# A hybrid streaming layer on one core: DVE instead of POOL takes the remainders of fourteen weight blocks behind the attention slots

## The chip, the cores and the metric

The kernel runs on one core of one Trainium2 chip. The metric is the device time of one execution in microseconds (us); lower is better. The engines are named as in the profile: PE multiplies matrices, PEld is its weight load, DVE is the vector engine, ACT the scalar engine, POOL is GpSimd, SP issues the transfers.

## The reference

One layer of an encoder serves two groups with the same weights: 512 new tokens without a past, and 64 tokens with 256 cached ones, together T = 576 columns of width 1024. Cut to the part around the change:

```
mixed = concat(rms_norm(fox_o, g_fox_out), rms_norm(mla_o, g_mla_out))
x = x + mixed @ w_o
q = (rms_norm(x, g_mem) @ w_mq)          # 4 heads x 128
s = q . mem_k * MEM_SCALE                # 256 memory tokens
o = softmax(s) @ mem_v
x = x + o @ w_mo
hf = rms_norm(x, g_ffn)
x = x + (silu(hf @ w_gate) * (hf @ w_up)) @ w_down
```

where mem_k and mem_v of the prompt are rms_norm(mem, g_mem_src) @ w_mk and @ w_mv. Before this stand the two attentions (fox_o and mla_o). All is float32 in and out.

## The kernel before, in words

**High and low parts.** Every float32 product is made of three passes of PE at the rounded type fp32r: high by high, high by low, low by high (`product`, L460 to L462). So each operand x needs a rounded copy (ACT) and the remainder x minus its rounded copy (DVE or POOL).

**Weight blocks.** The front weights come as 49 blocks of up to 128 x 1024 columns. SP loads block b into `wraw[b % 2]` (`load`, L2295) as soon as the remainder of block b - 2 is made (`f_lo` at b - 1). ACT rounds it into `whi[b % 3]` (`split`, waits for the load and for PE to be done with block b - 3, counts `f_hi`). `rest(b)` on POOL (L2125) makes the remainder `wlo[b % 3]` and counts `f_lo`. PE waits for `f_lo` at b + 1 before it uses block b. Blocks are taken in order.

**The stage around the change.** The attentions run in 96 ticks (to about 315 us in the profile); their last blocks are 31 and 32. Behind them stand, in PE's order: `mixed(0..7)`, the second half of w_o, two m to a block (blocks 32, 34, 36, 38), `memory_keys(3)` (33), `memory_values(0..3)` (35, 37, 39, 41), the first two heads' queries (40, 42), and then 20 slots of the memory attention (5 row tiles x 4 heads) with the queries of heads 2 and 3 (43, 44) and parts of `memout` (45 and on) as filler. After the slots come memout's blocks to 48 and the feed-forward part.

**DVE's order there.** For each m of the loop over `mixed`: scale the product in PSUM by the row factors (L1835), add it to `xa` (L1837), which counts `r_x`; then `low2(m - 1)` (L1818, the low part of the normed input; for m of 1 to 4) and `square_sum(m - 1)` (L1825, counts `r_acc`). ACT squares xa into the same PSUM pair and rounds it. `mixed(m)` for m over 3 waits for `r_acc` at m - 3, `query(0)` waits for `r_acc` at 6 (that is `square_sum(6)`) and then for `r_lo` part by part. In a slot s DVE takes the maximum (L1875), copies turned probabilities (L1882), and for slot s - 1 makes the reciprocal (L1893) and scales the probabilities (L1895, counts `m_sc`); PE turns slot s - 2 (`mturn`, L859) behind `m_sc`.

**POOL's order there.** `rest(33)` to `rest(38)`, `memory_key_lo(0)` and `(1)` (L2228, remainders of the memory keys: `kml`), `rest(39)`, `rest(40)`, `memory_key_lo(2)` and `(3)`, `rest(41)` to `rest(48)`. A `memory_key_lo` waits for ACT's rounded keys and for the store of the new memory keys to have landed (`s_mkst`). SP issues that store between `load(37)` and `load(38)`, behind `s_mkev` at 4.

Of the kernel before, what the change touches and what calls it, by code (L numbers as in the profile page):

```python
# [10 lines left out]
ALU = mybir.AluOpType  # L11
# [32 lines left out]
BLOCK_COLS = [768 if b < 4 or b in B_UQ else 1024 for b in range(B_FRONT)]  # L44
# [38 lines left out]
def tok(tt):  # L83

    return 128 if tt < 4 else TS


def build(nc, i_, o_, cum_dram):
# [3 lines left out]
    def place(name, shape, dt, at):  # L92
        size = int(np.prod(shape[1:])) * (2 if dt == BF16 else 4)
        assert at + size <= end, (name, at, size, end)
        return nc.alloc_sbuf_tensor_at(name, list(shape), dt, offset=at), at + (size + 31) // 32 * 32


    wraw, c = place("wraw", [128, 2, WB], F32, base)
    whi, c = place("whi", [128, 3, WB], F32R, c)
    wlo, c = place("wlo", [128, 3, WB], F32R, c)  # L100
# [124 lines left out]
    with ExitStack() as ctx:  # L225
# [3 lines left out]
        def sem(name):  # L229
            return ctx.enter_context(nc.semaphore(name))  # L230

        def two(pair):

            return ps[:, 2 * pair:2 * pair + 2, 0:HT]

        def rows2(bank):

            return flat[:, 512 * bank:512 * bank + T]

        def halves(ap):  # L240
            return ap.rearrange("p (a b) -> p a b", a=2)

        def f(ap):
            return ap.bitcast(F32)

        def need(eng, s, value, i=0, per=0):

            if isinstance(i, int):
                if value + per * i > 0:
                    eng.wait_ge(s, value + per * i)  # L250
            else:
                eng.wait_ge(s, i * per + value)

        f_load = [sem("f_load0"), sem("f_load1")]
        f_hi, f_lo = sem("f_hi"), sem("f_lo")
# [143 lines left out]
        def used(eng, b):  # L399

            if b in FILLER_END:
                eng.wait_ge(s_fdone, nth(FILLER_END[b]) + 1)
            else:
                past = [x for x in range(b % 3, b + 1, 3) if x not in FILLER_END]
                eng.wait_ge(f_used[b % 3], len(past))
# [23 lines left out]
        def mkept(t, u):  # L429
            if u == 4:  # L430
                return t[:, 1024:1152].rearrange("p (b q) -> p b q", q=TS)
            return t[:, 0:1024].rearrange("p (b q) -> p b q", q=512)[:, :, 128 * u:128 * u + 128]

        def mturned(s):
            return ps[:, s % 2, 0:256].rearrange("p (b q) -> p b q", q=128)[:, :, 0:tok(s % 5)]
# [5 lines left out]
        def half_a(c):  # L441

            return slice(64 * (c % 2), 64 * (c % 2) + 64)
# [1061 lines left out]
        def _(dve):  # L1505
            v = nc.vector

            def gain(g, j):
                return gains[:, g + j:g + j + 1]
# [115 lines left out]
            for tt in range(TT):  # L1625
                n = tok(tt)
# [127 lines left out]
            def memory_key(m):  # L1754

                used(dve, B_MK[m])
                v.tensor_tensor(kmf[:, m, 0:NM], ps[:, m, 0:NM], rmem[:, :], ALU.mult).then_inc(s_mkev, 1)
# [55 lines left out]
            memory_key(2)  # L1813
            dve.wait_ge(n_rs, 3)

            def low2(m):
                dve.wait_ge(r_hi, m + 1)
                v.scalar_tensor_tensor(hlo[:, m, :], xa[:, m, :], gain(G_MEM, m), f(hhi[:, m, :]),  # L1818
                                       ALU.mult, ALU.subtract).then_inc(r_lo, 1)

            def square_sum(m, at, count, source=None):

                dve.wait_ge(r_sq, at + m + 1)
                need(dve, r_acc, count + m - 1)
                v.tensor_tensor(halves(sqacc[:, 0:T]), halves(sqacc[:, 0:T]), source or halves(tmp2[:, m % 2, :]), ALU.add)\  # L1825
                    .then_inc(r_acc, 1)

            for m in range(8):
                if m % 2:
                    used(dve, B_WOM[m // 2])  # L1830
                else:
                    dve.wait_ge(s_gdone, 3 + m // 2)
                if m > 0:
                    dve.wait_ge(r_x, m)
                v.tensor_tensor(two(PAIR_WOM[m]), two(PAIR_WOM[m]), halves(rstd[:, :]), ALU.mult).then_inc(s_wmt, 1)  # L1835
                dve.wait_ge(s_wmt, m + 1)
                v.tensor_tensor(halves(xa[:, m, :]), halves(xa[:, m, :]), two(PAIR_WOM[m]), ALU.add).then_inc(r_x, 1)  # L1837
                if m == 1:
                    memory_key(3)
                if 1 <= m < 5:  # L1840
                    low2(m - 1)
                if m >= 2:
                    square_sum(m - 1, 0, 0, two(PAIR_WOM[m - 1]))
            square_sum(7, 0, 0, two(PAIR_WOM[7]))
            for m in range(4, 8):
                low2(m)

            def norm_rows(nth_, bank):
                dve.wait_ge(n_sd, nth_)
                v.reciprocal(small[:, S_RCC:S_RCC + 5], small[:, S_COL:S_COL + 5]).then_inc(n_rc, 1)  # L1850
                dve.wait_ge(n_row, nth_)
                v.tensor_copy(rstd[:, :], rows2(bank)).then_inc(n_rs, 1)
                dve.wait_ge(n_rs, nth_)
# [3 lines left out]
            def query(h):  # L1857
                used(dve, B_MQ[h])
                v.scalar_tensor_tensor(halves(mqf[:, h, :]), two(PAIR_MQ[h]), MEM_SCALE, halves(rstd[:, :]), ALU.mult, ALU.mult)\
                    .then_inc(s_mqev, 1)  # L1860

            def query_lo(h):
                dve.wait_ge(s_mqhi, h + 1)
                v.tensor_tensor(mql[:, h, :], mqf[:, h, :], f(mqh[:, h, :]), ALU.subtract).then_inc(s_mqlo, 1)

            for h in range(2):
                query(h)
                query_lo(h)
            for s in range(5 * MH + 6):
                h, u = s // 5, s % 5  # L1870
                if s < 5 * MH:
                    n = tok(u)
                    dve.wait_ge(m_qk, s + 1)
                    need(dve, m_ex, s - 4)
                    v.tensor_reduce(small[0:n, S_NMAX + u:S_NMAX + u + 1], ps[0:n, 2 + s % 2, 0:256], AX, ALU.max, negate=True)\  # L1875
                        .then_inc(m_mx, 1)
                if 3 <= s < 5 * MH + 3 and s % 2 == 0:
                    t = s - 3
                    dve.wait_ge(m_tr, t + 1)
                    if t >= 5:  # L1880
                        dve.wait_ge(m_pv if t % 5 == 4 else m_pv0, t // 5)
                    v.tensor_copy(mkept(mpt, t % 5), mturned(t)).then_inc(m_ptv, 1)  # L1882
                if s in (7, 12):
                    query(2 + s // 12)
                if s in (8, 13):
                    query_lo(2 + s // 13)
                if 1 <= s < 5 * MH + 1:
                    t = s - 1
                    h, u = t // 5, t % 5
                    n = tok(u)  # L1890
                    at, to = S_SUM + 10 * (h % 2) + 2 * u, S_COL + 5 * (h % 2) + u
                    dve.wait_ge(m_ex, t + 1)
                    v.reciprocal(small[0:n, to:to + 1], small[0:n, at:at + 1]).then_inc(m_ri, 1)  # L1893
                    dve.wait_ge(m_ri, t + 1)
                    v.tensor_scalar(mprobs[0:n, u, :], mprobs[0:n, u, :], small[0:n, to:to + 1], None, ALU.mult).then_inc(m_sc, 1)  # L1895
                if s in (10, 15, 20, 25):
                    h = s // 5 - 2
                    dve.wait_ge(m_ohi, h + 1)
                    v.tensor_tensor(molo[:, h, :], rows2(6), f(mohi[:, h, :]), ALU.subtract).then_inc(m_olo, 1)
# [218 lines left out]
        def _(pool):  # L2118
            g = nc.gpsimd

            def rest(b):

                n = BLOCK_COLS[b]
                pool.wait_ge(f_hi, b + 1)
                g.tensor_tensor(wlo[:, b % 3, 0:n], wraw[:, b % 2, 0:n], f(whi[:, b % 3, 0:n]), ALU.subtract).then_inc(f_lo, 1)  # L2125
# [25 lines left out]
            def query_lo(c):  # L2151

                a = half_a(c)
                if c in (0, 2, 4, 6):
                    pool.wait_ge(f_lo, {0: 14, 2: 16, 4: 19, 6: 21}[c])
                pool.wait_ge(x_qhi, c + 1)
                g.tensor_tensor(q1[c % 4][half_b(c), :], qt[a, :], f(q1[c % 4][a, :]), ALU.subtract).then_inc(x_qlo, 1)
                pool.wait_ge(x_qlo, c + 1)
# [68 lines left out]
                pool.wait_ge(s_mkst, 16)  # L2227
                g.tensor_tensor(kml[:, m, :], kmf[:, m, :], f(kmh[:, m, :]), ALU.subtract).then_inc(s_mklo, 1)  # L2228

            for b in range(33, 39):  # L2230
                rest(b)
            memory_key_lo(0)
            memory_key_lo(1)
            rest(39)
            rest(40)
            memory_key_lo(2)
            memory_key_lo(3)

            rest(41)
            rest(42)  # L2240
            for b in range(43, 49):
                rest(b)

            def remainder(c):

# [370 lines left out]
```

## Time and profile before

| | us |
|---|---|
| median of three runs | 844.51 (843.86 to 844.65) |
| the profiled execution, its own time | 844.28 |
| its span from first to last instruction | 842.5 |
| mean granted clock of TensorE, share of full speed | 0.991 |
| PE busy in the span | 814.2 (97%) |
| DVE, ACT, POOL busy | 538.4, 397.9, 367.4 |

The time of the profiled execution is the span and 1.8 us around it. PE's busy time is that of overlapping matmuls, so where it is full PE has always something in flight; the share says where PE had gaps. Idle time of an engine that nobody waits for costs nothing.

### The profile page before, as it was taken

The page shows a single profiled execution, that of the slowest core. Times are in us where ns is not written, and L with a number is a line of the kernel's source. Part 1 is how long each engine was busy: PE and PEld are TensorE (multiplying, and loading weights), DVE is VectorE, ACT ScalarE, POOL GpSimd, SP SyncE. Part 2 cuts the span into 40 slices and gives each one's busy share as a digit, 9 for nine tenths or more (in the row PEclk, how much of TensorE's full clock was granted, in tenths as well). Part 3 has the DMA queues.
Part 4 walks back from the last instruction along what each step waited for, and adds up shares of the span by engine and source line. Part 5 has one row for each costly group of instructions (what it writes and reads, how often), then busy time and mean ns, then how long its engine had stood idle before and what let it go on. Part 6 is the DMA issues. An engine that isn't in the chain of part 4 may idle for free.

```text
span 842.5 us, 16025 instructions
## 1 busy us (share of the span) xinstructions
PE 814.2 (97%) x5913; PEld 768.5 (91%) x5913; DVE 538.4 (64%) x911; ACT 397.9 (47%) x735; POOL 367.4 (44%) x213
## 2 busy tenths in 40 slices
PE   6999999989999999999999999999999999999995
PEld 6987998878887899988799999999999999999995
DVE  5244466666557855637588998898988887212214
ACT  6433564656566435445545455544555555222210
POOL 2652864546325453751195333333333345533420
PEclk9999999999999999999999999999999999999998
DMA  7332422100123334341032232222232332323103
GB/s 260 101 110 84 154 91 66 60 1 21 51 76 138 100 102 125 100 126 51 1 121 81 101 100 87 73 89 100 100 100 100 100 101 73 107 85 93 46 1 113
DMA packets 26392, 75.49 MB, mean 90 GB/s; under 512 B 3025, under 2 KB 7449, under 8 KB 26201
## 3 DMA queue, kind: packets, MB, share of 16 engines
q1 hardware_dynamic: 26336, 74.74, 27.9%
q8 instruction: 37, 0.61, 0.3%
q14 instruction: 19, 0.15, 0.1%
HBM read 68.20 MB, written 6.53 MB: 89 GB/s over the span
## 4 chain that ended last, share of the span: by engine, by line
PE 84%; DVE 7%; issue 3%; POOL 2%; ACT 2%; DMA 1%; SPq 0%; DVEq 0%; ACTq 0%
PE ps L460 26%; PE ps L461 24%; PE ps L462 24%; PE ps L612 2%; PE ps L630 2%; POOL hf L2252 1%; PE ps L874 1%; PE ps L478 1%; DVE tf L1923 1%; PE ps L591 1%; PE ps L590 1%; ACT whi L1055 1%; DMA wraw<-w_front 1%; POOL wlo L2247 1%; PE ps L596 1%
## 5 line engine op out<-in xcount | busy, mean ns | idle before, releaser
L460 PE MATMUL ps<-hhi,whi 128*128 128x288 f32 x896 | 269.7, 301 | 12.0 <-DVE hlo L1528 6.7
L461 PE MATMUL ps<-hhi,wlo 128*128 128x288 f32 x896 | 265.9, 297 | 0.0
L462 PE MATMUL ps<-hlo,whi 128*128 128x288 f32 x800 | 237.4, 297 | 0.0
L2125 POOL TENSOR_TENSOR wlo<-wraw,whi 128x1024 fp32r<-128x1024 f32 (+1 forms) x48 | 113.5, 2369 | 174.0 <-ACT whi L1055 173.8
L460 PEld LDWEIGHTS ps<-hhi,whi 128*128 128x128 f32 x896 | 169.9, 190 | 15.2 <-issue 10.1
L1055 ACT ACTIVATE whi<-wraw 128x1024 fp32r<-128x1024 f32 (+3 forms) x138 | 114.6, 838 | 136.1 <-PE ps L462 121.5
L461 PEld LDWEIGHTS ps<-hhi,wlo 128*128 128x128 f32 x896 | 169.5, 189 | 0.2
L462 PEld LDWEIGHTS ps<-hlo,whi 128*128 128x128 f32 x800 | 151.2, 189 | 0.0
L2271 POOL TENSOR_TENSOR wlo<-wraw,whi 128x512 fp32r<-128x512 f32 x60 | 78.8, 1327 | 150.4 <-ACT whi L1055 150.4
L462 PE MATMUL ps<-hidlo,whi 128*128 128x288 f32 x352 | 103.9, 295 | 0.0
L2285 POOL TENSOR_TENSOR wlo<-wraw,whi 128x1024 fp32r<-128x1024 f32 (+1 forms) x24 | 59.3, 2477 | 72.9 <-ACT whi L1055 72.9
L1675 DVE TENSOR_REDUCE small<-ps 128x1 f32<-128x128 f32 (+4 forms) x80 | 39.0, 487 | 58.9 <-PE ps L596 53.6
L462 PE MATMUL ps<-tl,whi 128*128 128x288 f32 x240 | 71.4, 297 | 0.0
L461 PE MATMUL ps<-th,wlo 128*128 128x288 f32 x240 | 71.3, 297 | 0.0
L460 PE MATMUL ps<-th,whi 128*128 128x288 f32 x240 | 70.9, 295 | 0.0
L1055 ACT ACTIVATE whi<-ss 128x512 fp32r<-128x512 f32 x61 | 38.4, 631 | 63.6 <-PE ps L462 35.4
L462 PEld LDWEIGHTS ps<-hidlo,whi 128*128 128x128 f32 x352 | 66.1, 188 | 0.0
L1055 ACT ACTIVATE probs<-ps,small 128x128 f32<-128x128 f32 (+4 forms) x80 | 41.9, 524 | 42.8 <-DVE small L1675 42.0
L2075 DVE TENSOR_TENSOR tmp<-ps,rstd 128x576 f32<-128x576 f32 (+1 forms) x9 | 6.2, 691 | 85.9 <-PE ps L462 85.9
L460 PE MATMUL ps<-hidhi,whi 128*128 128x288 f32 x192 | 56.9, 296 | 0.0
L461 PE MATMUL ps<-hidhi,wlo 128*128 128x288 f32 x192 | 56.8, 296 | 0.0
L460 PEld LDWEIGHTS ps<-th,whi 128*128 128x128 f32 x240 | 45.2, 188 | 0.0
(287 smaller groups left out, 1814.4 us busy)
## 6 DMA issues: line engine op xcount, KB each, us to landing
wraw<-w_ff SPq DMA_DIRECT2D x44, 512.0 KB, 4.1
wraw<-w_front SPq DMA_DIRECT2D x41, 512.0 KB, 3.6
wraw<-w_down SPq DMA_DIRECT2D x16, 512.0 KB, 3.7
wraw<-w_down SPq DMA_DIRECT2D x8, 384.0 KB, 3.1
wraw<-w_front SPq DMA_DIRECT2D x7, 384.0 KB, 3.6
xs<-x_t SPq DMA_DIRECT2D x8, 288.0 KB, 5.7
xa<-x_t SPq DMA_DIRECT2D x8, 288.0 KB, 4.6
out_y<-xb SPq DMA_DIRECT2D x16, 144.0 KB, 1.9
```

What stands on the lines that cost most here:

```text
L460: nc.tensor.matmul(out, lh, rh, start=start, stop=False)
L461: nc.tensor.matmul(out, ll, rh, start=False, stop=False)
L462: return nc.tensor.matmul(out, lh, rl, start=False, stop=stop)
L478: mm = nc.tensor.matmul(ps[:, bank, at + tt:at + tt + 1], source[:, 128 * tt:128 * tt + 128], ones[:, 0:1], start=True, stop=True)
L590: nc.tensor.matmul(out, q1[r][:, q], k1[r][:, ks], start=True, stop=False)
L612: mm = nc.tensor.transpose(ps[:, 2 + s % 2, 128 * kb:128 * kb + 128], probs[:, P_AT[u] + 128 * kb:P_AT[u] + 128 * kb + 128], ident[:, :])
L630: mm = nc.tensor.matmul(ps[64 * e:64 * e + 64, 4, 128 * kb:512], va[:, g, kb, h + e, :], pt[e][:, 512 * kb:512 * kb + 512 - 128 * kb], sta ...
L1055: return nc.scalar.activation(out, src, func, **kw)
L1675: v.tensor_reduce(nmax, ps[0:n, s % 2, 0:w], AX, ALU.max, negate=True).then_inc(s_mx, 1)
L2125: g.tensor_tensor(wlo[:, b % 3, 0:n], wraw[:, b % 2, 0:n], f(whi[:, b % 3, 0:n]), ALU.subtract).then_inc(f_lo, 1)
L2271: g.tensor_tensor(w_operand(1, j), src, f(w_operand(0, j)), ALU.subtract).then_inc(g_lo, 1)
L2285: g.tensor_tensor(ffw(n, 1, 1, w)[:, 0, :], (wraw2, wraw)[n % 4 // 2][:, n % 2, 0:w], f(ffw(n, 0, 1, w)[:, 0, :]), ALU.subtract).then_inc( ...
```

## The change

`rest(33)` to `rest(46)` leave POOL's program. DVE does the same subtraction on the same tiles in a new function `weight_rest`, called at fixed places of its program: 33 and 34 before the loop over `mixed`; 35 and 36, 37 and 38, 39 and 40 in the loop's rounds m = 2, 4 and 6, ahead of `low2` and `square_sum`; 41 and 42 after the last `low2`; 43 between the memory queries 0 and 1; 44, 45 and 46 in the slots 2, 4 and 8 of the memory attention. POOL keeps the four `memory_key_lo`, now one behind the other, and `rest(47)` and `rest(48)`, ahead of which it waits for `f_lo` at 47.

```diff
+            def weight_rest(b):
+
+                n = BLOCK_COLS[b]
+                dve.wait_ge(f_hi, b + 1)
+                dve.wait_ge(f_lo, b)
+                v.tensor_tensor(wlo[:, b % 3, 0:n], wraw[:, b % 2, 0:n], f(whi[:, b % 3, 0:n]), ALU.subtract).then_inc(f_lo, 1)
+
+            weight_rest(33)
+            weight_rest(34)
...
                 if m == 1:
                     memory_key(3)
+                elif m in (2, 4, 6):
+                    weight_rest(33 + m)
+                    weight_rest(34 + m)
                 if 1 <= m < 5:
                     low2(m - 1)
...
             for m in range(4, 8):
                 low2(m)
+            weight_rest(41)
+            weight_rest(42)
...
-            for h in range(2):
-                query(h)
-                query_lo(h)
+            query(0)
+            query_lo(0)
+            weight_rest(43)
+            query(1)
+            query_lo(1)
...
+                if s in (2, 4, 8):
+                    weight_rest(43 + s // 2 - s // 8)
                 if s in (7, 12):
                     query(2 + s // 12)
...
-            for b in range(33, 39):
-                rest(b)
             memory_key_lo(0)
             memory_key_lo(1)
-            rest(39)
-            rest(40)
             memory_key_lo(2)
             memory_key_lo(3)
 
-            rest(41)
-            rest(42)
-            for b in range(43, 49):
-                rest(b)
+            pool.wait_ge(f_lo, 47)
+            rest(47)
+            rest(48)
```

DVE's order in rounds m = 4 to 7 of the loop over `mixed`, before (L1835 scales the product, L1837 adds it to xa, L1818 is low2, L1825 is square_sum):

```order
L1835 TENSOR_TENSOR ps<-ps,rstd 128x2x288
L1837 TENSOR_TENSOR xa<-xa,ps 128x576
L1818 SCALAR_TENSOR_TENSOR hlo<-xa,gains,hhi 128x576
L1825 TENSOR_TENSOR sqacc<-sqacc,ps 128x576
L1835 TENSOR_TENSOR ps<-ps,rstd 128x2x288
L1837 TENSOR_TENSOR xa<-xa,ps 128x576
L1825 TENSOR_TENSOR sqacc<-sqacc,ps 128x576
L1835 TENSOR_TENSOR ps<-ps,rstd 128x2x288
L1837 TENSOR_TENSOR xa<-xa,ps 128x576
L1825 TENSOR_TENSOR sqacc<-sqacc,ps 128x576
```

The same rounds of the change (up to the end of round 6), where those lines are L1845, L1847, L1828 and L1835, and L1821 is `weight_rest`:

```order
L1845 TENSOR_TENSOR ps<-ps,rstd 128x2x288
L1847 TENSOR_TENSOR xa<-xa,ps 128x576
L1821 TENSOR_TENSOR wlo<-wraw,whi 128x1024 x2
L1828 SCALAR_TENSOR_TENSOR hlo<-xa,gains,hhi 128x576
L1835 TENSOR_TENSOR sqacc<-sqacc,ps 128x576
L1845 TENSOR_TENSOR ps<-ps,rstd 128x2x288
L1847 TENSOR_TENSOR xa<-xa,ps 128x576
L1835 TENSOR_TENSOR sqacc<-sqacc,ps 128x576
L1845 TENSOR_TENSOR ps<-ps,rstd 128x2x288
L1847 TENSOR_TENSOR xa<-xa,ps 128x576
L1821 TENSOR_TENSOR wlo<-wraw,whi 128x1024 x2
L1835 TENSOR_TENSOR sqacc<-sqacc,ps 128x576
```

Two subtractions of 128 x 1024 stand between the addition to xa and the square sum in rounds 4 and 6 (and 2), so that `low2` and `square_sum` come after them.

POOL's order from the last attention ticks on, before (L2125 is `rest`, L2228 `memory_key_lo`; the first two of the x8 are blocks 31 and 32, the last two of the other x8 are 47 and 48):

```order
L2218 TENSOR_TENSOR sqacc<-sqacc,tmp_60 128x576
L2125 TENSOR_TENSOR wlo<-wraw,whi 128x1024 x8
L2228 TENSOR_TENSOR kml<-kmf,kmh 128x512 x2
L2125 TENSOR_TENSOR wlo<-wraw,whi 128x1024 x2
L2228 TENSOR_TENSOR kml<-kmf,kmh 128x512 x2
L2125 TENSOR_TENSOR wlo<-wraw,whi 128x1024 x8
L2252 TENSOR_SCALAR hf<-xb,gains 128x576 x3
```

The same stretch of the change, with `rest` at L2144 and `memory_key_lo` at L2247:

```order
L2237 TENSOR_TENSOR sqacc<-sqacc,tmp_60 128x576
L2144 TENSOR_TENSOR wlo<-wraw,whi 128x1024 x2
L2247 TENSOR_TENSOR kml<-kmf,kmh 128x512 x4
L2144 TENSOR_TENSOR wlo<-wraw,whi 128x1024 x2
L2266 TENSOR_SCALAR hf<-xb,gains 128x576 x3
```

The four `kml` remainders no longer stand behind six and two weight blocks; nothing is ahead of them but their own waits. The orders of PE, ACT and SP are the same in both kernels.

## Rows read from the trace of the kernel before

**Rows 1.** The page's busy times: us, share of the span, instructions.

```profile
PE 814.2 (97%) x5913; PEld 768.5 (91%) x5913; DVE 538.4 (64%) x911; ACT 397.9 (47%) x735; POOL 367.4 (44%) x213
```

**Rows 2.** Busy time of each engine by stage: loop over mixed, queries, slots.

```profile
core 0: us, PE busy (x) PEld busy (x) DVE busy (x) ACT busy (x) POOL busy (x), PEclk, DMA share, GB/s
315.00:345.00 30.00, 29.39 (x204) 27.88 (x203) 17.32 (x23) 14.26 (x20) 15.74 (x8) 1.00 0.41 123
345.00:371.00 26.00, 26.00 (x179) 24.60 (x178) 10.51 (x15) 11.47 (x16) 16.23 (x8) 1.00 0.36 106
371.00:395.00 24.00, 23.09 (x165) 20.96 (x164) 16.59 (x43) 13.22 (x35) 5.26 (x3) 1.00 0.27 85
```

**Rows 3.** Waits of PE, 315 to 371 us: us in total, times, longest.

```profile
PE ps L460 <- DVE kmf L1757: 0.6, 1, 0.6
```

**Rows 4.** Timeline of POOL: start, us, instruction, idle before.

```profile
326.27 4.74 POOL L2125 TENSOR_TENSOR wlo<-wraw,whi 128x1024 fp32r<-128x1024 f32 x2 [7.60 <-ACT whi L1055]
341.04 3.07 POOL L2228 TENSOR_TENSOR kml<-kmf,kmh 128x512 fp32r<-128x512 f32 x2
376.09 2.40 POOL L2125 TENSOR_TENSOR wlo<-wraw,whi 128x1024 fp32r<-128x1024 f32 x1 [4.59 <-ACT whi L1055]
```

**Rows 5.** The group of DVE's subtraction of 512 columns, and the four kml.

```profile
L1957 DVE TENSOR_TENSOR ss<-wraw,ss 128x512 f32<-128x512 f32 x1 | 0.7, 692 | 0.0
L2228 POOL TENSOR_TENSOR kml<-kmf,kmh x4: 1286/1298/1812, 341.0 to 351.5; 128x512 fp32r<-128x512 f32 x4
```

**Rows 6.** Timelines of DVE and POOL at the start of the feed-forward part.

```profile
453.77 2.21 DVE L1923 TENSOR_TENSOR tf<-hf 128x1152 f32<-128x1152 f32 x1
456.09 2.26 DVE L1923 TENSOR_TENSOR tf<-hf,tf 128x1152 f32<-128x1152 f32 x1
459.54 1.35 DVE L1923 TENSOR_TENSOR tf<-hf,tf 128x1152 f32<-128x1152 f32 x1
...
453.48 3.66 POOL L2271 TENSOR_TENSOR wlo<-wraw,whi 128x512 fp32r<-128x512 f32 x2 [3.39 <-ACT whi L1055]
```

**Rows 7.** Timeline of DVE in rounds 2, 4 and 6 of the loop.

```profile
329.96 0.75 DVE L1837 TENSOR_TENSOR xa<-xa,ps 128x576 f32<-128x576 f32 x1
...
339.86 1.83 DVE L1818 SCALAR_TENSOR_TENSOR hlo<-xa,gains,hhi 128x576 fp32r<-128x576 f32 x1
341.62 0.74 DVE L1825 TENSOR_TENSOR sqacc<-sqacc,ps 128x576 f32<-128x576 f32 x1
...
347.64 0.77 DVE L1835 TENSOR_TENSOR ps<-ps,rstd 128x576 f32<-128x576 f32 x1 [3.15 <-PE ps L462]
349.11 0.75 DVE L1825 TENSOR_TENSOR sqacc<-sqacc,ps 128x576 f32<-128x576 f32 x1
```

**Rows 8.** Timeline of SP, and the landing of the store of the keys.

```profile
328.69 0.33 SPq L2295 DMA_DIRECT2D wraw<-w_front  x1
329.06 0.60 SPq L2411 DMA_DIRECT2D out_mem_k<-kmf  x1
...
DMA to landing us min/median/max: 5.0/5.0/5.0
```

**Rows 9.** Timeline of PE: first matmuls of mixed(6) and of query(0).

```profile
344.22 0.30 PE L460 MATMUL ps<-hhi,whi 128*128 128x288 f32 x1
...
353.47 0.30 PE L460 MATMUL ps<-hhi,whi 128*128 128x288 f32 x1
```

**Rows 10.** Timelines of DVE and PE in the slots 2 to 8.

```profile
377.22 1.42 DVE L1895 TENSOR_SCALAR mprobs<-mprobs,small 128x256 f32<-128x256 f32 x1
379.41 0.35 DVE L1895 TENSOR_SCALAR mprobs<-mprobs,small 128x256 f32<-128x256 f32 x1
384.52 1.69 DVE L1895 TENSOR_SCALAR mprobs<-mprobs,small 128x256 f32<-128x256 f32 x1
...
380.14 0.39 PE L859 MATMUL ps<-ident,mprobs 128*128 128x128 f32 x2
```

## The prediction

> **What bounds the kernel now.** I read the page first. PE is busy for 97% of the span, DVE for 64%, POOL for 44% [rows 1]; so DVE has room on average, and the kernel goes by PE. The average says little about one stage, so next the stretches by stage [rows 2]: in the loop over `mixed` PE is busy 29.4 of 30 us, through the queries 26.0 of 26, and in the slots with filler 23.1 of 24. The list of waits names for 315 to 371 us one wait of PE, 0.6 us for DVE's last memory keys [rows 3], and none for POOL. So the weight remainders of POOL are not late anywhere here: POOL makes two blocks in 4.74 us and sits idle for 7.6 us before them, because ACT has nothing rounded for it [rows 4]. A faster maker of remainders has nothing to give PE in this stage. What can move the time is what the new work does to DVE's own clients, whose margins I take from the timelines of DVE, PE, POOL and SP, one round at a time.
>
> **What one moved subtraction costs.** POOL takes 2.37 us (half of 4.74) [rows 4]. DVE has no 128 x 1024 in the trace. It takes 0.69 us for 512 columns of the same kind [rows 5] and 1.35 us for 1152 [rows 6]; the line between them gives 1.22 us for 1024. Its lower bound is 1.20 (1.35 in proportion to the columns), its upper one 1.38 (twice 0.69). I take 1.22. Fourteen of them are 17 us of DVE, 33 us off POOL. `weight_rest` also waits for the one before it to be counted, 0.04 us.
>
> **Both engines share something.** On DVE the instructions with two operands in SBUF stretch when a subtraction of POOL runs. The low part at 339.86 us takes 1.83 us and ends 0.6 us after POOL's weight block, which ends where its kml starts, at 341.04 [rows 4, 7]; the scaling at 377.22 takes 1.42 us and ends with POOL's block of 376.09 to 378.49 (0.35 us in its plain form at 379.41) [rows 4, 10]. And they take turns: POOL's two subtractions, 1.28 us each when alone (that is the shortest kml, of the same 512 columns [rows 5]), take 3.66 us from 453.48, while DVE's two of 1152 columns take 2.21 and 2.26 instead of 1.35 [rows 6]. That is POOL, DVE, POOL, DVE: neither gets two in a row while the other stands waiting. From rows 4 and 7 a turn costs the one who waits about so much: POOL's pair of kml ends at 344.11, so the first ended at 342.8, 1.15 us after DVE's low part (341.69).
>
> The Trainium skill (SBUF — State Buffer, section "Who interferes with whom") states this: a DVE instruction with two inputs in SBUF contends with a GpSimd instruction that reads SBUF, and the second to issue fully blocks. It speaks for the change where POOL's blocks leave DVE alone, and against it where the new DVE instructions, all of this kind, meet what POOL keeps; who goes first when both have queued up it does not say, and by DVE going first the stall of round 4 below would be nothing, by turns 1.7 us. The rows above show turns.
>
> **Rounds m = 0 and 2.** Blocks 33 and 34 fit into DVE's idle time ahead of round 0. In round 2 the addition ends at 330.71 [rows 7], so block 35 is done at 331.9 instead of 328.6 (the first half of POOL's 4.74 from 326.27) [rows 4], block 36 at 333.1 instead of 331.0. PE takes block 35 at about 332.2, so this holds by 0.2 us. But SP's next load waits for block 35's remainder (it left at 328.69), and behind it in SP's queue stands the store of the memory keys, 0.37 us later, 5.0 us to its landing [rows 8]. It goes from 329.06 to 332.3 and lands at 337.3 instead of 334.1. POOL's four kml, now with nothing ahead of them, wait for that: the first two run from 337.3 to 339.9, the other two stand ready when ACT has rounded keys 2 and 3 (about 341). That is just when DVE comes to round 4.
>
> **Round m = 4, stall A.** DVE's addition ends at 339.9, as before [rows 7]. Block 37 ends at 341.1 (POOL's second kml is just out of the way). The third kml stands waiting: to 342.2. Block 38: 1.05 more, 343.3. Fourth kml: to 344.4. `low2(3)` ends 0.6 later, at 345.1, `square_sum(3)` at 345.8. `mixed(6)` waits for it, and PE started it at 344.22 [rows 9]; with 0.15 us from count to matmul it starts at 345.9: 1.7 us. Without turns the same sum is 339.86 + 1.26 + 1.22, low part 0.81, square sum 0.74 with their overlaps: 343.7, and no stall. In the kernel before the square sum ended at 342.36 [rows 7]. If the store lands half a microsecond earlier or later, A is 1.1 or 2.3.
>
> **Round m = 6, stall B.** Here nothing of POOL's is in the way. In the old count DVE comes to the next step at 349.11 [rows 7]. Two blocks take it to 351.59, `square_sum(5)` ends at 352.2, scaling and adding m = 7 take 1.48 (347.64 to 349.11 is the same pair) to 353.7, `square_sum(6)` ends at 354.4. `query(0)` waits for that one; PE started it at 353.47 [rows 9] and would start at 354.55: 1.1 us. Before, DVE had idle time between m = 6 and 7, which hid all but the sum itself. The later low parts (0.7 us each against PE's 0.8 us a step) don't add to it. Both stalls add up, since after A everything of this stage is shifted alike.
>
> **Queries, blocks 41 to 43.** DVE waits for PE and ACT here, more than the 3.7 us that these take (10.5 of 26 us busy [rows 2]): nothing.
>
> **Slots, C.** Block 44 in slot 2 makes the scaled probabilities of slot 1 about 0.1 us late for PE. Block 45 in slot 4 puts those of slot 3, done at 379.76, to 380.4; PE turns them at 380.14 [rows 10]: about 0.3. Block 46 in slot 8 takes the place of the 1.3 us for which POOL's block held up the scaling of 384.52 [rows 10]: nothing. What is given back, 1.07 and 1.34 us of held-up DVE, ends in front of a PE that is busy with filler; its only return is 0.1 us where PE came for the row of 377.22. C is 0.3, at least 0, at most the whole of two blocks, 2.4.
>
> **Behind it.** Blocks 47 and 48 and what follows keep their engines and their order, and hang on PE's memout; nothing there absorbs a shift. The sum: 1.7 + 1.1 + 0.3 = 3.1 us on the profiled 844.28, 847.4. The median of the runs is 0.23 above the profiled execution: 847.6.
>
> **The rivals.**
> *DVE isn't held up in round 4*: kml 2 and 3 come late, or DVE gets two turns. For it: turns show only once, and ACT's last rounded key is as late as 341. Then A is 0, and B + C give 1.4: 845.9. Chance 0.24.
> *DVE's hold-ups set the pace (the other side)*: the three instructions that POOL's blocks hold up, by 1.0, 1.07 and 1.34 us (339.86, 377.22 and 384.52 [rows 7, 10]), make PE late by as much in ways that the list of waits doesn't show, and come back whole, 3.4 us, as POOL's blocks are gone. Against B's 1.1 that leaves 2.3: 842.2. It decides as soon as more comes back than A and B take; against it, PE is busy for 23.1 of 24 us in the slots [rows 2]. Chance 0.08.
> *The softmax chain sets the pace*: both blocks 44 and 45 cost PE their whole 1.22 us instead of 0.3 together: 847.6 + 2.1 = 849.7. For it: DVE is already 16.6 of 24 us busy [rows 2] and its steps hang on each other. Chance 0.10.
> *Nothing to be seen*: PE's queue hides A and most of B, as margins of 0.2 to 1 us are too fine to be taken from one trace; 844.5 to 845.5. Chance 0.08.
> The forecast itself, A and B both there, has 0.50.
>
> **How the numbers follow.** A measurement of this kernel tells about 0.2%, 1.7 us, from no change: the bounds are 842.8 and 846.2. Slower: the forecast 0.50, the paced softmax 0.10, and a quarter of the first rival (845.9 is close to the bound), 0.06: 0.66. Within: 0.18 + 0.08 = 0.26. Faster 0.08. The forecast alone runs from A = 1.1, B = 0.8, C = 0 to A = 2.3, B = 1.3, C = 0.8: 846.4 to 848.9. The range takes in the first rival below and half of the paced softmax above: 845.2 to 849.2.
>
> **What would show it.** The waits of PE name DVE's sqacc (the square sum, L1835) before `mixed(6)` with over 1 us and before `query(0)` with about 1 us. The store of the keys is issued near 332 us; the kml stand between 337 and 345, two of them stretched to about 2 us, a `weight_rest` of block 38 as well. `weight_rest` alone is 1.22 us. In the slots the scaling has no row over 1 us any more. Wrong would be: a kml cluster before 336 or behind 346, a start of `query(0)` 9.25 us behind that of mixed(6), as before (344.22 and 353.47), or PE waiting in round 2 for block 35.

## The result and the profile after

| | before | after |
|---|---|---|
| median, us | 844.52 (843.86 to 844.65, 4 runs) | 849.21 (848.06 to 850.43, 4 runs) |
| ratio, 95% interval | | 1.0059, 1.0047 to 1.0072 |
| profiled execution, its own time | 844.28 | 848.06 |
| its span | 842.5 | 846.3 |

The change makes the kernel 4.7 us slower. I had forecast 847.6 with a range to 849.2: the direction was right, the time lies above the range by a hair, and the size is 1.6 us more than the 3.1 of my sum.

The page's busy times of the changed kernel, which answer to [rows 1]:

```profile
PE 815.2 (96%) x5913; PEld 767.4 (91%) x5913; DVE 551.3 (65%) x925; ACT 398.0 (47%) x735; POOL 335.0 (40%) x199
```

The work has gone where it should. POOL has 32 us less and DVE 13 more: 19 us in the fourteen subtractions (17, and 2 in which they stood behind POOL's), less 3.6 us by which its scalings in the slots and its low parts are shorter without POOL's blocks beside them, and less 1.9 us in casts near 100 us, which the change doesn't touch. The waits of PE from 312 to 416 us, who waited for whom, us in total, times, longest:

```profile
PE ps L460 <- DVE sqacc L1835: 1.5, 2, 0.9
PE ps L859 <- DVE mprobs L1914: 1.3, 4, 0.5
PE ps L460 <- DVE wlo L1821: 0.7, 1, 0.7
PE ps L460 <- DVE kmf L1757: 0.6, 1, 0.6
```

Up to 371 us only the last was there before [rows 3]; of the wait for `mprobs`, all of it in the slots, the kernel before has 1.0 us in three. The three matmuls that waited newly there are, in the timeline of PE, memory_values(1), mixed(6) and query(0):

```profile
341.01 0.50 PE L460 MATMUL ps<-whi,memh 128*128 128x512 f32 x1 [0.70 <-DVE wlo L1821]
344.72 0.37 PE L460 MATMUL ps<-hhi,whi 128*128 128x288 f32 x1 [0.64 <-DVE sqacc L1835]
...
355.07 0.41 PE L460 MATMUL ps<-hhi,whi 128*128 128x288 f32 x1 [0.90 <-DVE sqacc L1835]
```

This execution came to the loop 1.27 us earlier than the one of before: DVE's copy of the row factors ahead of round 0 starts at 314.44 instead of 315.71, in a part that the change doesn't touch. So I compare distances. From that copy to mixed(6) it was 28.51 us (344.22 in [rows 9]), now it is 30.28: 1.77 more. From there to query(0) it was 9.25, now 10.35: 1.10 more. These distances, and not the waits, give the loss: the waits of 0.70 and 0.64 us count only the time in which PE had nothing left in flight, while memory_values(1) starts 0.87 us late (26.57 after the copy instead of 25.70).

Why mixed(6) is late, DVE's timeline of round 4 and POOL's of the key remainders:

```profile
337.92 0.76 DVE L1847 TENSOR_TENSOR xa<-xa,ps 128x576 f32<-128x576 f32 x1
338.59 4.59 DVE L1821 TENSOR_TENSOR wlo<-wraw,whi 128x1024 fp32r<-128x1024 f32 x2
343.11 0.81 DVE L1828 SCALAR_TENSOR_TENSOR hlo<-xa,gains,hhi 128x576 fp32r<-128x576 f32 x1
343.84 0.74 DVE L1835 TENSOR_TENSOR sqacc<-sqacc,ps 128x576 f32<-128x576 f32 x1
...
369.31 1.22 DVE L1821 TENSOR_TENSOR wlo<-wraw,whi 128x1024 fp32r<-128x1024 f32 x1
...
336.07 6.03 POOL L2247 TENSOR_TENSOR kml<-kmf,kmh 128x512 fp32r<-128x512 f32 x4 [29.02 <-DMA out_mem_k<-kmf]
```

Two subtractions, of 1.22 us each where alone (369.31), take 4.59 us, and the four of POOL 6.03 instead of some 5.1. They stand beside each other from 338.59 on: DVE's take 2.37 and 2.13 us, and POOL's last one 2.27. POOL was released by the landing of the store of the keys, as foreseen; DVE's square sum ends at 344.58 and PE starts 0.14 us later.

Behind the slots there is something new. Busy times and granted clock of 8 us there, in both kernels from 4.4 us before POOL's block 47, so that the same work stands in the same row. First the changed kernel:

```profile
core 0: us, PE busy (x) PEld busy (x) DVE busy (x) ACT busy (x) POOL busy (x), PEclk, DMA share, GB/s
407.24:411.24 4.00, 2.78 (x18) 1.67 (x17) 3.31 (x11) 2.47 (x6) 0.00 (x0) 1.00 0.00 0
411.24:415.24 4.00, 4.00 (x10) 2.23 (x11) 0.00 (x0) 0.22 (x1) 2.34 (x1) 0.57 0.02 4
```

and the kernel before:

```profile
405.00:409.00 4.00, 2.79 (x18) 1.67 (x16) 3.25 (x11) 2.40 (x6) 0.00 (x0) 1.00 0.00 0
409.00:413.00 4.00, 4.00 (x22) 3.04 (x23) 0.24 (x2) 0.95 (x2) 2.35 (x1) 1.00 0.02 4
```

The third column from the right is the clock: 1.00 is 2.4 GHz, and 0.57 a mean of 3.4 us at 1.2 GHz and the rest at 2.4. In the second stretch 10 matmuls ran instead of 22. In the first one, ahead of the fall, PE's busy time is the same in both kernels, 2.78 and 2.79 us of 4.

### The profile page after: what moved, and what is told of

The parts are those of the page before. It is cut to its first block, busy times and chain, and to the rows that moved or that the text cites. A ratio compares the mean times of both kernels' runs of the same rounds, so it can differ in the third digit from the quotient of the medians.

```text
span 846.3 us, 16039 instructions
## 1 busy us (share of the span) xinstructions
PE 815.2 (96%) x5913; PEld 767.4 (91%) x5913; DVE 551.3 (65%) x925; ACT 398.0 (47%) x735; POOL 335.0 (40%) x199
## 4 chain that ended last, share of the span: by engine, by line
PE 82%; DVE 8%; issue 3%; POOL 2%; ACT 2%; DMA 1%; SPq 0%; DVEq 0%; ACTq 0%
PE ps L460 25%; PE ps L461 24%; PE ps L462 24%; PE ps L612 2%; PE ps L630 2%; POOL hf L2266 1%; PE ps L874 1%; PE ps L478 1%; ACT whi L1055 1%; DVE tf L1942 1%; DMA wraw<-w_front 1%; PE ps L591 1%; PE ps L590 1%; POOL wlo L2261 1%; PE ps L596 1%
## 5 line engine op out<-in xcount | busy, mean ns | idle before, releaser
L2144 POOL TENSOR_TENSOR wlo<-wraw,whi 128x1024 fp32r<-128x1024 f32 (+1 forms) x34 | 80.3, 2362 | 181.2 <-ACT whi L1055 181.0
L2299 POOL TENSOR_TENSOR wlo<-wraw,whi 128x1024 fp32r<-128x1024 f32 (+1 forms) x24 | 59.4, 2478 | 72.9 <-ACT whi L1055 72.9
```

What stands on the lines that cost most here:

```text
L2299: g.tensor_tensor(ffw(n, 1, 1, w)[:, 0, :], (wraw2, wraw)[n % 4 // 2][:, n % 2, 0:w], f(ffw(n, 0, 1, w)[:, 0, :]), ALU.subtract).then_inc( ...
```

## How the times were taken apart

The trace has four points that every kernel passes: DVE's copy of the row factors ahead of round 0, DVE's scaling of memory query 1 (behind both stalls), POOL's block 47 (behind the slots) and POOL's block 48. Their starts, as distances in us, for the profiles of this study, with the places at which the granted clock fell to half, for 3.4 us or, where it says "long", for 6.8. One more fall, at the very end, is in all of them and left out; it begins 5.0 to 8.9 us before the last instruction, and the last distance spreads with it.

```
kernel                        start to copy  to query 1  to block 47  to 48   to end   clock falls near
before                          315.71        55.55       38.11       10.45   422.68   60, 172
before, again                   316.53        55.54       38.11       10.44   422.58   60, 172 long
before, third                   315.32        55.55       38.08       10.42   422.43   172
change                          314.44        58.47       38.70       12.04   422.65   60, 412
change, again                   314.62        58.36       38.70       12.08   422.64   60, 412
change, third                   317.64        58.44       38.69       10.36   422.87   60, 172 long
blocks 33-42 only               314.28        58.40       38.10       10.43   422.49   none
blocks 33-42 only, again        314.62        58.40       38.10       10.44   422.34   60
blocks 33-42 only, third        316.99        58.41       38.10       10.46   422.64   60, 172 long
blocks 43-46 only               314.44        55.54       38.69       12.04   422.99   60, 410
blocks 43-46 only, again        314.33        55.53       38.68       12.01   422.85   60, 410
key remainders late             315.25        56.68       38.70       11.98   423.09   172, 412
odd rounds                      315.49        55.49       38.69       10.38   422.35   172
all in idle time                313.89        55.54       38.37       12.05   422.95   410
```

The middle distances repeat to 0.1 us from one execution to the next where the clock does not fall. The falls don't all cost the same: the one near 410 costs 1.6 us (12.04 instead of 10.44), the one near 60 some 0.4 (314.33 to 314.62 to the copy with it alone, 313.89 and 314.28 with none), the one near 172 some 1.3 (315.25 to 315.49 with it alone), and where it is long, beside the one near 60, the copy is reached at 316.53 to 317.64. So small terms can be read from single profiles, while the runs' times spread by 4 us.

## The experiments

The first four ran together beside 25 runs of the kernel before (844.17), the next two beside 23 (844.33).

**Blocks 33 to 42 alone on DVE** (the loop's part of the change):

```diff
-                if s in (2, 4, 8):
-                    weight_rest(43 + s // 2 - s // 8)
...
-            weight_rest(43)
...
-            pool.wait_ge(f_lo, 47)
-            rest(47)
-            rest(48)
+            pool.wait_ge(f_lo, 43)
+            for b in range(43, 49):
+                rest(b)
```

> DVE makes blocks 33 to 42 only, POOL 43 to 48. Theory (each stall adds: 1.8 us in rounds 2 to 4 by DVE and POOL taking turns, 1.1 us at query(0) by too much work on DVE in round 6; the slots cost 0.6 us; a fall of PE's clock near 412 us costs 1.6 us when it occurs): both stalls in the waits of PE, about +2.9 us, 847.4. If the clock falls here too, +4.5. Rival (the slots cost what the change loses, the two stalls are made up later): within 1 us of the kernel before.

846.91 us (845.51 to 848.50, 7 runs), ratio 1.0036 (1.0022 to 1.0050), 2.7 us over the kernel before. Its waits of PE name the same two causes as the change's:

```profile
PE ps L460 <- DVE sqacc L1835: 1.5, 2, 0.9
PE ps L460 <- DVE wlo L1821: 0.6, 1, 0.6
```

By the table it loses 2.85 us up to query 1 and nothing behind, in each of its three profiles. The stalls are not made up later.

**Blocks 43 to 46 alone on DVE** (the slots' part): the subtractions before, in and behind the loop go back to POOL, in the order of the kernel before.

```diff
-            weight_rest(33)
-            weight_rest(34)
...
-                elif m in (2, 4, 6):
-                    weight_rest(33 + m)
-                    weight_rest(34 + m)
...
-            weight_rest(41)
-            weight_rest(42)
```

> DVE makes blocks 43 to 46 only, POOL the rest as before. Theory: +0.6 us (block 44 and 45 each put PE's turning of probabilities off by a few tenths), 845.1, and no fall of the clock that the kernel before doesn't have, unless the slots are what brings it on: then +2.2 us and a granted clock near half in some 3 us behind the slots. Rival (the softmax chain sets the pace): +2.4 us without a fall of the clock.

845.39 us (843.82 to 846.51, 12 runs), ratio 1.0012 (1.0002 to 1.0022). By the table the slots cost 0.58 us, not 2.4: the softmax chain does not set the pace. And the clock fell behind them, which cost this execution 1.6 us more. The stretches before, at and after it:

```profile
395.00:404.00 9.00, 8.52 (x49) 6.37 (x49) 7.62 (x24) 5.73 (x19) 0.00 (x0) 1.00 0.00 1
404.00:412.00 8.00, 6.78 (x27) 3.96 (x26) 3.31 (x11) 2.79 (x8) 2.35 (x1) 0.80 0.01 2
412.00:416.00 4.00, 4.00 (x30) 3.74 (x29) 0.76 (x1) 0.65 (x1) 0.00 (x0) 0.98 0.00 0
```

**The key remainders late.** The change, with one wait more on POOL:

```diff
+            pool.wait_ge(f_lo, 43)
             memory_key_lo(0)
```

> The changed kernel, in which POOL makes the four key remainders only after block 42's remainder, so that they meet no DVE subtraction. Theory (turns for the port): the two subtractions of round 4 take 2.5 us instead of 4.6, the waits of PE before memory_values(1) and mixed(6), 1.8 us in all, are gone, the one before query(0) stays at about 1.1 us: 1.8 us faster than the change, 847.4. Rival (DVE has too much work in round 4 in any case): the wait moves to mixed(6) and the time stays at 849.

847.33 us (843.83 to 850.11, 12 runs), ratio 1.0029 (1.0014 to 1.0044). DVE's round 4, and the key remainders, which now stand far behind it:

```profile
339.40 2.55 DVE L1821 TENSOR_TENSOR wlo<-wraw,whi 128x1024 fp32r<-128x1024 f32 x2
341.87 0.81 DVE L1828 SCALAR_TENSOR_TENSOR hlo<-xa,gains,hhi 128x576 fp32r<-128x576 f32 x1
...
360.34 5.00 POOL L2247 TENSOR_TENSOR kml<-kmf,kmh 128x512 fp32r<-128x512 f32 x4 [52.48 <-DVE wlo L1821]
```

and its only long wait of PE:

```profile
354.05 0.40 PE L460 MATMUL ps<-hhi,whi 128*128 128x288 f32 x1 [0.87 <-DVE sqacc L1835]
```

The pair takes 2.55 instead of 4.59 us, both waits of round 4 are gone, and the one before query(0) is left, 1.13 us by the table (56.68 less 55.55). So the 1.8 us of stall A go when the two engines' subtractions no longer lie on each other: in this place two subtractions alone cost PE nothing. (That the overlap by itself costs nothing either, two experiments on shows.)

**The change again**, for its clock and its spread:

> The changed kernel again. Theory: 849 as before, PE's clock falls to half behind the slots (near 412 us) in the profiled execution again if it is the change that brings it on; if the fall is by chance, it is missing in some executions, which are then 1.6 us faster, near 847.5.

848.16 us (846.14 to 849.31, 7 runs), ratio 1.0043 (1.0028 to 1.0058). The fall near 412 us is there a second time; in a third profile, further down, it is not.

**The subtractions of the loop in odd rounds**, behind `square_sum`, where DVE had idle time:

```diff
-                elif m in (2, 4, 6):
-                    weight_rest(33 + m)
-                    weight_rest(34 + m)
...
                 if m >= 2:
                     square_sum(m - 1, 0, 0, two(PAIR_WOM[m - 1]))
+                if m in (1, 3, 5):
+                    weight_rest(34 + m)
+                    weight_rest(35 + m)
```

> The changed kernel with the six subtractions of the loop moved to the end of rounds 1, 3 and 5, where DVE stood idle for 2.9 to 3.2 us in the kernel before; blocks 41 to 46 as in the change. Theory (what costs is only that the subtractions stand ahead of work that PE waits for): no wait of PE before mixed(6), memory_values(1) and query(0), left are the slots' 0.5 us; at an equal granted clock 2.7 us faster than the change. Rival (DVE has too much work in the stage, or its subtractions meet POOL's key remainders wherever they stand): a wait of about 1 us stays.

845.41 us (844.25 to 847.05, 12 runs), ratio 1.0014 (1.0002 to 1.0025). From 315 to 371 us PE waits once, for what it waited for before:

```profile
PE ps L460 <- DVE kmf L1757: 0.6, 1, 0.6
```

In round 3 DVE and POOL still meet: the pair takes 4.15 us, and DVE goes on without a gap, some 2 us later than in the kernel before:

```profile
336.06 4.15 DVE L1821 TENSOR_TENSOR wlo<-wraw,whi 128x1024 fp32r<-128x1024 f32 x2 [0.91 <-ACT whi L1055]
340.13 0.75 DVE L1845 TENSOR_TENSOR ps<-ps,rstd 128x576 f32<-128x576 f32 x1
```

But now no subtraction stands between the addition of round 4 and the square sum, which ends 0.9 us before mixed(6) starts (343.06 and 344.00), and mixed(6) starts 28.51 us after the copy, as in the kernel before. Both stalls are gone (55.49 to query 1). So what they cost was the place of the subtractions, not their number.

**All of them in idle time.** As the last one, and the blocks of the slots moved:

```diff
             weight_rest(43)
+            weight_rest(44)
             query(1)
...
-                if s in (2, 4, 8):
-                    weight_rest(43 + s // 2 - s // 8)
+                if s in (8, 13):
+                    weight_rest(45 + s // 13)
```

> As the one before, and block 44 before the memory query 1, 45 in slot 8 and 46 in slot 13. Theory: nothing of the slots' 0.5 us is left, so the kernel before within 0.1% at an equal granted clock, or up to 0.2 us faster for the scaling that POOL no longer holds up. If the fall of the clock near 412 us comes from the stall in slots 2 and 4, it is missing. Rival (it comes from POOL or DVE idle or busy there): it shows here too.

844.66 us (843.35 to 846.41, 12 runs), ratio 1.0009 (0.9997 to 1.0021): no difference that can be told. Half of the slots' cost is gone (38.37 to block 47, 0.27 over before); the rest I had expected gone too. The trace shows where it comes from: block 46, now at 395.30 us in slot 13, makes the next scalings late, and PE waits for one of them.

```profile
395.30 1.22 DVE L1821 TENSOR_TENSOR wlo<-wraw,whi 128x1024 fp32r<-128x1024 f32 x1
398.82 0.44 PE L859 MATMUL ps<-ident,mprobs 128*128 128x128 f32 x2 [0.32 <-DVE mprobs L1915]
```

Up to there PE is 0.1 us ahead of the kernel before (counted from query 1), which is all that comes back of the 3.4 us by which POOL had held up DVE. The clock fell here as well, with no stall left in slots 2 and 4:

```profile
408.00:412.00 4.00, 4.00 (x12) 2.11 (x10) 0.00 (x0) 0.00 (x0) 2.15 (x1) 0.58 0.01 4
```

That expectation, that the fall comes with the stall in slots 2 and 4, has failed.

**Six more profiles for the clock**, of kernels already shown: before twice more, blocks 33 to 42 twice, blocks 43 to 46 once, the change once.

> The kernel before once more, for its profile alone. If the fall of the clock near 412 us belongs to the subtractions in the slots, it is missing here; those near 60 and 172 us may come or not. If it is by chance, it shows in about every second execution of any kernel.

> The kernel with DVE's blocks 33 to 42 only, once more, for its profile alone. As for the kernel before: no fall near 412 us if it belongs to the slots, though the two stalls of the loop are there.

> DVE makes blocks 43 to 46, POOL the rest, once more, for its profile alone. If the fall of the clock near 412 us goes with blocks 44 to 46 being off POOL (so far 5 of 6 such profiles have it, 0 of 4 others), it shows here. If it is by chance, one in two.

> The changed kernel a third time, for its profile alone: the fall near 412 us shows if it goes with blocks 44 to 46 being off POOL. The waits of PE are as in the first two: 0.9 and 0.6 in round 4, 0.9 before query(0).

> The kernel before a third time, for its profile alone: no fall near 412 us if that goes with the blocks of the slots; one in two if it is by chance.

> The kernel with DVE's blocks 33 to 42 only a third time, for its profile alone: no fall near 412 us if that goes with the blocks of the slots; one in two if it is by chance.

Their single times are 844.99, 845.69, 845.19, 849.79, 843.61 and 848.47 us. Falls near 410: blocks 43 to 46 yes, the other five no, the change's third among them. That one is the slowest of the three all the same, since its clock fell near 172 and for twice as long, 6.8 us:

```profile
170.00:178.00 8.00, 6.41 (x23) 5.91 (x24) 4.03 (x10) 4.09 (x11) 7.09 (x5) 0.57 0.00 0
```

It came to the copy 3.2 us later than the profile of the result, which has no fall near 172.

## Why the prediction was right and where it was wrong

**What bounds the kernel, and that POOL was not late: right.** With the work at the right places (odd rounds, all in idle time) nothing is gained; without POOL's fourteen blocks PE does not get through this stage faster.

**One subtraction, 1.22 us: right.** It is 1.22 where alone.

**Stall A, 1.7 us: right in size and cause, in part at another place.** It measured 1.77. The store was issued at 330.99 and POOL's key remainders start at 336.07, which is 332.3 and 337.3 when the 1.27 us are put back, as worked out. But the first turn went to POOL: PE came to block 37 0.87 us late, and the pair took 4.59 us where my sum had 3.4 (339.9 to 343.3). So both of the last two key remainders lay ahead of or within the pair and none met `low2(3)` (0.81, not stretched). The end is nearly the same, for either way DVE stands behind POOL twice; that it is the same to 0.1 us is in part luck. The loss is split into 0.87 us before memory_values(1) and 0.90 before mixed(6), so the sign that I had named, a wait of over 1 us before mixed(6), did not come (0.64). Late keys took all of it away; turns are thus what the trace shows for this pair too.

**Stall B, 1.1 us: right**, 1.10 in the change and 1.13 with late keys. The sum of DVE's work between mixed(6) and query(0) was enough for it.

**Slots, C: too small.** I had 0.3, measured 0.59. Counted from query 1, PE's turning of slot 1 was 0.12 us late and that of slot 3 0.48 in all, near the 0.1 and 0.3 of my steps before I took 0.1 off for the scaling that POOL no longer holds up; the remaining 0.1 came in later slots.

**"Nothing there absorbs a shift": this step failed, for something there adds to one.** My sum goes on behind the slots with zero, without a reason why the clock should stay. In the profile of the result PE's clock fell there to 1.2 GHz for 3.4 us, and between blocks 47 and 48 the distance is 12.04 instead of 10.45 us, 1.6 us. With it the profiles add up: 2.92 and 0.59 and 1.59 make 5.1, less the 1.27 that this execution had gained ahead of the copy, give the 3.8 by which the spans differ. It had gained them since its clock did not fall near 172, where that of before did.

How far this belongs to the change is the weak point. Over the profiles with at least blocks 44 to 46 off POOL the fall near 410 shows in 6 of 8, over the others in 0 of 6; if the six falls were dealt to the 14 profiles at random, they would all go to those eight in 28 of 3003 ways, about once in a hundred. But that way of parting the profiles was found by looking at them; of the last four, taken to test it, three came out as it says and the change's third did not. The fall comes without the stall in slots 2 and 4, and PE's busy time in the 4 us ahead of it is the same in the kernel before (2.79 us) and in the change's third profile (2.78), where none comes. In the two where it is missing the clock fell near 172, but with late keys it fell at both places. The runs point the same way: the mean granted clock of the whole execution was 0.9895 over the change's first four runs and 0.9916 over the next seven, against 0.9928 over 48 runs of the kernel before. A linear fit of time against kernel and clock over the 114 timed runs of these kernels gives 0.47 us for each 0.001 of clock (what it leaves spreads by 0.5 us), and at the same clock the change costs 3.4 us, blocks 33 to 42 2.9, blocks 43 to 46 0.6, late keys 1.9, odd rounds 0.9, all in idle time 0.2 (each give or take 0.4). So 3.4 us of the loss are the terms of my sum with C mended, shown one by one; the other 1.3 us are clock, seen in the runs, with the cause open. The miss itself hangs on that: the first four runs had the lowest mean clock of all groups, the seven later ones have a median of 848.16, inside my range.

**The rivals.** DVE not held up in round 4 is what happens with late keys, not in the change. The other side fell: POOL's hold-ups of DVE are gone (no scaling in the slots is over 0.35 us) and it shows in 0.1 us of PE in the slots and in no run's time. The paced softmax fell too (0.59, not 2.4), though it named a time near the measured one; a range that had a clock fall of 1.6 us in it would have held.

## What to carry to other kernels

Before work is moved to an engine that is idle a third of the time, sum up what that engine does between two of its results that the bounding engine waits for: two subtractions fitted into the stage and not into one round, while the same six behind the square sum cost nothing. An instruction left behind on the old engine moves too: it starts when its own last wait ends, here a store that the change itself had delayed, and lands on the new work. And a difference under 1% is read from distances between fixed points of the trace, with the clock's falls noted beside them.

## What the runs showed of the hardware

DVE's and POOL's subtractions, each with two operands in SBUF, exclude each other: a pair on DVE takes 2.55 us alone and 4.59 or 4.15 beside POOL's. The Trainium skill (SBUF — State Buffer, section "Who interferes with whom") says so, and these traces agree. In a tie neither engine got a second turn: POOL's four of about 1.25 us took 6.03 us around DVE's two.

PE's granted clock falls to half for 3.4 us, near 172 us also for 6.8, at a few places of this program (near 60, 172 and 410 us), now at one and now at another; the one near 410 costs 1.6 us, the one near 60 some 0.4. The 48 runs of one and the same kernel lie between 841.67 and 846.33 us, and their medians go with the mean clock: 842.9 at 0.995, 844.3 at 0.993, 844.9 at 0.991, 845.7 at 0.989. Ahead of the one near 172 PE has gaps, but the same gaps stand there without a fall. The stretch ahead of it in the execution of before, which had the fall:

```profile
165.00:172.00 7.00, 4.49 (x31) 3.56 (x30) 6.77 (x13) 4.75 (x13) 6.53 (x6) 1.00 0.01 3
```

and in that of the change, which had none:

```profile
165.00:172.00 7.00, 4.51 (x32) 3.55 (x32) 6.74 (x13) 5.05 (x13) 6.53 (x6) 1.00 0.04 16
```

What else decides it, none of these runs shows.
